# Differential attention two heads at a time: its PE steps put between the halves of a weight chunk, and the vector engine's norm put ahead of two splits

## The chip, the cores and the metric

The kernel runs on one core of a Trainium2 chip. The metric is the device time of one execution in microseconds (us), the median of several runs. Engines are named as the profile names them: PE is the matrix engine and PEld its weight load, DVE the vector engine, ACT the scalar engine, POOL the GpSimd engine, SP the engine that issues most of the weight DMAs.

## What is computed

The reference is a trunk of two layers over 256 tokens of width 2048. Layer 0 mixes tokens by differential attention, layer 1 by dilated sliding-window attention, and each is followed by a gated feed-forward block with a causal convolution. The change touches layer 0's attention and its output projection only:

```python
def diff_attention(h, w_qkv, q_gain, k_gain, lam, subln_g, w_o, rel_bias, layer_idx):
    qkv = h @ w_qkv                                   # 256 x 2048 by 2048 x 6144
    q, k, v = jnp.split(qkv, [nqk, 2 * nqk], axis=-1)
    q = rmsnorm(q.reshape(B, S, N_HEADS, 2, HEAD_DIM), q_gain)
    k = rmsnorm(k.reshape(B, S, N_HEADS, 2, HEAD_DIM), k_gain)
    ...
    logits = q k^T * scale + bias                     # causal, two maps for each head
    p = jax.nn.softmax(logits, axis=-1)
    a = p[:, :, 0] - lam_full * p[:, :, 1]
    o = a @ v
    o = rmsnorm(o, subln_g) * (1.0 - lam_init)
    return o.reshape(B, S, ATTN_WIDTH) @ w_o
```

There are 8 heads with a query and a key of 2 x 128 and a value of 256 columns. Everything is float32, and the products are made to float32 accuracy.

## The kernel before

**How a product is made.** A weight chunk is a slab of 128 partitions x 2048 float32. It lands in one of the four slots of w_raw, ACT rounds it into w_hi (the *high part*, `split_b`, L682, or `split`, L658), and DVE makes the remainder w_lo = w_raw - w_hi (the *low part*, also `split_b`, L1144, or `split`, L1126). The activations xT are kept as a high and a low half in the same way. PE multiplies the high part by both halves of xT (16 matmuls of 512 columns) and then the low part by the high half (8 matmuls). So a plain chunk is 24 matmuls, and it waits twice: for w_hi at its start (`hi_ready`), for w_lo two thirds of the way through (`lo_ready`). A slot of w_raw is loaded again when DVE has made its w_lo; ACT may overwrite w_hi when PE has used the chunk (`used`).

**A pair of heads.** `a_pair` runs over four pairs p = 0 to 3. Each pair has 15 chunks, numbered e = 0 to 14 here as in the code: four "all" chunks for the values (e = 0 to 3, `moving`, matmuls L1902, L1903 and L1909), then eleven for queries and keys (L2053 and L2057). Six of these eleven are mixed as in Strassen's scheme: "one" chunks (9 matmuls) and "sum" chunks (12 matmuls), whose sums of weights DVE makes (`add_weights`, L1162 to L1167). Queries and keys of the two heads come out in four psum banks; after chunk 13 ACT takes one product out (`a_take_p1`, L737), DVE makes four combinations (`a_combine`, L1290 to L1295), and after chunk 14 DVE adds four sums (`a_sum`, L1302). The values come out in two banks after chunk 3 and are scaled into a_v (`a_take_v`: one bank by ACT at L730, the other by DVE at L1281). The lower two banks of chunk 4 can't be written before that (`lower_free` in `upper_first`).

**The attention of pair p - 1 runs beside the chunks of pair p** (`a_attend`, in each engine's program; behind the last pair it runs beside the output projection `a_out_proj`). A_STEPS says after which chunk PE does each of its five steps: transposes of q and k (L1922, waits for `a_qkn`), scores (L1930 and L1933), transposes of the probabilities (L1938), probabilities by values (L1944 to L1946), transposes of the output (L1952). The other engines' parts hang on the same numbers:

```python
A_STEPS = (1, 2, 5, 6, 8)
A_LAST_STEPS = (1, 2, 5, 6, 8)
```

ACT squares the sums at e = 0 (`a_squares`, L744), takes q out at step 0 (L749), does the exponentials at step 1 (`a_exp`, L757) and takes the transposed probabilities at step 2 (L764). DVE normalises q and k at e = 0 (`a_norm`: a reduction at L1307, twelve small instructions, and a product over 128 x 2048 at L1315 that sets `a_qkn`), takes k out at step 0 (L1319), does logits and maxima at step 1 (`a_softmax`, L1331 to L1345), and the weighted difference of the two maps at the entry after it (`a_subtract`).

**Order.** There is no scheduler: each engine's program is written out, and an engine does its instructions in that order. In pair p, ACT and DVE make the parts of chunk e + 3 at entry e (`split_ahead`), before the attention step of that entry. So on DVE the norm (e = 0) stands behind the low part of the pair's chunk 3, and `a_combine` of the pair before stands behind the low part of chunk 1.

**The seam.** `a_out_proj` makes 16 chunks of the output projection: j = 0 to 5 into the left half, 6 to 8 into a third quarter, 9 and 10 left again, 11 third, 12 to 15 the fourth. PE begins it when `a_combined` has come for the last pair. Chunk 9 needs the heads of the last pair, after their transposes (step 4) and `split_o` (L838 on ACT, L1433 on DVE). The third quarter's banks 4 and 5 were also those of the transposed probabilities, so PE waits for `a_aT_ready` ahead of chunk 6.

## Time and profile before

| | us |
|---|---|
| median of 3 runs | 2536.39 (2534.1 to 2538.67) |
| the profiled execution | 2531.31, of which the span is 2529.5 |
| PE busy | 2489.1 (98%) |
| DVE busy | 2165.6 (86%) |
| ACT busy | 1469.0 (58%) |
| DMA | mean 194 GB/s |

The profile is one execution. The span runs from the first to the last instruction; the rest of the execution's time lies around it. Layer 0's attention with its output projection takes the first 440 us of the span; the four pairs' chunks begin at about 24, 77, 161 and 248 us, the output projection at 335 us. PE and PEld overlap. The ends of matmuls are modelled, so a row's idle time can be some tenths of a us short of the distance between two matmuls.

### The profile page before, as it was taken

Reading aid. Unit: us, or ns where it says so; the run is one execution under the profiler, and the core shown is the slowest. Engines: PE = TensorE matmul, PEld = TensorE weight load, DVE = VectorE, ACT = ScalarE, POOL = GpSimd, SP = SyncE. Lnnn points to the kernel's source line nnn. Section 1 sums busy time; section 2 is a strip of 40 time slices with the busy share of each in tenths; the row PEclk is TensorE's granted clock in tenths of the full one; section 3 lists DMA queues with packets and bytes.
Section 4 is the critical chain, followed back from the end, with each engine's and each line's share of the span. In section 5 each row is a group of like instructions: output and inputs, shape, how many; then the busy total and the mean of one; then the engine's idle time right before and its main releaser. Section 6 shows DMA issues by size and latency. Waiting matters only on the chain.

```text
span 2529.5 us, 29120 instructions
## 1 busy us (share of the span) xinstructions
PE 2489.1 (98%) x11403; PEld 2069.2 (82%) x11403; DVE 2165.6 (86%) x2393; ACT 1469.0 (58%) x1432; POOL 44.2 (2%) x54
## 2 busy tenths in 40 slices
PE   9899899999999999999999999999999999999999
PEld 8777777888888888888888888888888888888887
DVE  7777685899999999998787887777599999999998
ACT  6445454767675755565554554544567676665654
POOL 1000000000000000000000000000000000000000
PEclk9999999999999999999999999999999999999999
DMA  8563355567676755665666666555467676755654
GB/s 286 168 195 132 106 183 183 167 221 224 205 231 200 240 177 194 204 224 170 185 185 197 188 185 174 161 162 194 147 213 229 200 239 200 243 189 200 231 172 162
DMA packets 359401, 491.24 MB, mean 194 GB/s; under 512 B 20005, under 2 KB 200437, under 8 KB 356832
## 3 DMA queue, kind: packets, MB, share of 16 engines
q1 hardware_dynamic: 355024, 465.64, 56.1%
q0 software_dynamic: 4000, 23.63, 4.3%
q8 instruction: 90, 1.47, 0.2%
q14 instruction: 47, 0.39, 0.0%
q10 hardware_dynamic: 240, 0.10, 0.0%
HBM read 468.31 MB, written 3.68 MB: 187 GB/s over the span
## 4 chain that ended last, share of the span: by engine, by line
PE 91%; DVE 5%; ACT 2%; issue 1%; DMA 1%; SPq 0%; ACTq 0%; DVEq 0%
PE psum L2053 46%; PE psum L2057 23%; PE psum L1902 5%; PE psum L1903 5%; PE psum L1909 5%; PE psum L2156 2%; DMA w_raw<-in_a_w_qkv 1%; PE psum L2283 1%; DVE w_lo L1144 1%; ACT w_hi L682 1%; PE psum L1922 0%; PE psum L2247 0%; PE psum L2281 0%; PE psum L1860 0%; PE psum L2255 0%
## 5 line engine op out<-in xcount | busy, mean ns | idle before, releaser
L2053 PE MATMUL psum<-w_hi,xT 128*128 128x512 f32 x4456 | 1117.6, 391 | 8.6 <-ACT phase L730 8.6
L2053 PEld LDWEIGHTS psum<-w_hi,xT 128*128 128x128 f32 x4456 | 834.0, 188 | 181.5 <-ACT phase L730 9.8
L669 ACT ACTIVATE w_hi<-w_raw 128x2048 fp32r<-128x2048 f32 (+1 forms) x350 | 631.1, 1810 | 389.6 <-PE psum L2057 257.2
L1136 DVE TENSOR_TENSOR w_lo<-w_raw,w_hi 128x2048 fp32r<-128x2048 f32 (+1 forms) x332 | 705.1, 2145 | 57.4 <-ACT w_hi L669 57.0
L2057 PE MATMUL psum<-w_lo,xT 128*128 128x512 f32 x2228 | 585.1, 390 | 1.0 <-DVE w_lo L1144 0.9
L2057 PEld LDWEIGHTS psum<-w_lo,xT 128*128 128x128 f32 x2228 | 418.8, 188 | 90.1 <-DVE w_lo L1144 2.2
L1144 DVE TENSOR_TENSOR w_lo<-w_raw,w_hi 128x2048 fp32r<-128x2048 f32 (+1 forms) x174 | 376.5, 2178 | 66.8 <-ACT w_hi L682 66.2
L682 ACT ACTIVATE w_hi<-w_raw 128x2048 fp32r<-128x2048 f32 (+1 forms) x174 | 316.0, 1827 | 141.3 <-PE psum L2057 79.5
L2053 PE MATMUL psum<-w_hi,mixT 128*128 128x512 f32 x992 | 265.3, 389 | 0.0
L1902 PE MATMUL psum<-w_hi,xT 128*128 128x512 f32 x624 | 248.9, 399 | 10.2 <-DVE phase L1295 5.0
L1903 PE MATMUL psum<-w_hi,xT 128*128 128x512 f32 x624 | 245.1, 393 | 0.0
L2053 PEld LDWEIGHTS psum<-w_hi,mixT 128*128 128x128 f32 x992 | 186.2, 188 | 38.9
L1909 PE MATMUL psum<-w_lo,xT 128*128 128x512 f32 x624 | 154.2, 389 | 0.0
L1162 DVE TENSOR_TENSOR w_raw<-w_raw 128x1024 f32<-128x1024 f32 x124 | 151.2, 1219 | 2.7 <-DMA w_raw<-in_f_w_down 1.7
L2057 PE MATMUL psum<-w_lo,mixT 128*128 128x512 f32 x496 | 153.1, 390 | 0.0
L1902 PEld LDWEIGHTS psum<-w_hi,xT 128*128 128x128 f32 x624 | 118.6, 190 | 36.9 <-DVE phase L1295 5.4
L1903 PEld LDWEIGHTS psum<-w_hi,xT 128*128 128x128 f32 x624 | 118.7, 190 | 24.0
L1909 PEld LDWEIGHTS psum<-w_lo,xT 128*128 128x128 f32 x624 | 117.1, 188 | 24.3
L1126 DVE TENSOR_TENSOR w_lo<-w_raw,w_hi 128x2048 fp32r<-128x2048 f32 x38 | 86.0, 2288 | 27.9 <-ACT w_hi L658 27.9
L2057 PEld LDWEIGHTS psum<-w_lo,mixT 128*128 128x128 f32 x496 | 92.9, 188 | 20.0 <-DVE w_lo L1144 0.7
L1167 DVE TENSOR_TENSOR w_raw<-w_raw 128x512 f32<-128x512 f32 x124 | 85.8, 692 | 4.2
L1165 DVE TENSOR_TENSOR w_raw<-w_raw 128x512 f32<-128x512 f32 x124 | 85.8, 692 | 4.2
(204 smaller groups left out, 1803.7 us busy)
## 6 DMA issues: line engine op xcount, KB each, us to landing
w_raw<-in_f_w_up SPq DMA_DIRECT2D x352, 512.0 KB, 5.0
w_raw<-in_f_w_down SPq DMA_DIRECT2D x176, 512.0 KB, 5.1
w_raw<-in_b_w_qkv SPq DMA_DIRECT2D x192, 256.0 KB, 3.8
w_raw<-in_a_w_qkv SPq DMA_DIRECT2D x132, 256.0 KB, 4.2
w_raw<-in_b_w_qkv SPq DMA_DIRECT2D x256, 128.0 KB, 2.6
w_lo<-w_raw POOLq DMA_DIRECT2D x18, 1024.0 KB, 7.1
w_raw<-in_a_w_o SPq DMA_DIRECT2D x16, 1024.0 KB, 5.3
w_raw<-in_b_w_qkv SPq DMA_DIRECT2D x32, 512.0 KB, 6.1
```

Of the source, the lines that this page charges most:

```text
L669: nc.scalar.activation(w_hi[:, slot, cols], w_raw[:, slot, cols], ACT.Copy).then_inc(hi_ready, 1)
L682: nc.scalar.activation(w_hi[:, slot, cols], w_raw[:, slot, cols], ACT.Copy).then_inc(hi_ready, 1)
L1126: nc.vector.tensor_tensor(w_lo[:, slot, :], w_raw[:, slot, :], w_hi[:, slot, :], ALU.subtract).then_inc(lo_ready, 1)
L1136: nc.vector.tensor_tensor(w_lo[:, slot, cols], w_raw[:, slot, cols], w_hi[:, slot, cols], ALU.subtract).then_inc(lo_ready, 1)
L1144: nc.vector.tensor_tensor(w_lo[:, slot, cols], w_raw[:, slot, cols], w_hi[:, slot, cols], ALU.subtract).then_inc(lo_ready, 1)
L1162: chain.step(nc.vector.tensor_tensor(t[:, 0:2, :], b[:, 1::2, :], b[:, 0:1, :].to_broadcast([P, 2, 512]), ALU.add))
L1165: chain.step(nc.vector.tensor_tensor(t[:, 2, :], t[:, 0, :], b[:, 3, :], ALU.add))
L1902: pe.matmul(o, xh, hi, start=(first and i == 0), stop=False)
L1903: pe.matmul(o, xl, hi, start=False, stop=False)
L1909: ins = pe.matmul(psum[:, banks[m], 0:n], xT[:, k, 0, P * m:P * (m + 1)], lo, start=False, stop=(last and i == len(blocks) - 1))
L2053: pe.matmul(o, x[:, h, P * m:P * (m + 1)], hi, start=start and h == 0, stop=False)
L2057: return pe.matmul(o, x[:, 0, P * m:P * (m + 1)], part_of(w_lo, c % SLOTS, 512 * tile, 512), start=False, stop=stop)
```

## The change

It has these parts, all in layer 0's attention and output projection:

- **Steps moved.** A_STEPS becomes (2, 3, 5, 6, 8) and A_LAST_STEPS (2, 3, 5, 6, 7): the transposes of q and k and the scores come one chunk later, the last pair's output transposes one chunk earlier. With them go ACT's and DVE's parts.
- **Between the parts of a chunk.** `moving` gets a function `between` that it calls behind the 16 matmuls with the high part and ahead of the wait for the low part. A_BETWEEN and A_LAST_BETWEEN say which steps stand there: the q and k transposes and the scores, and at the seam also probabilities by values.
- **DVE's order at the turn of a pair.** `a_combine` now stands ahead of the low part of chunk 1, that low part stands behind `a_sum`, and the norm stands ahead of the low parts of chunks 2 and 3. For e < 5 the attention step stands ahead of the split, not behind it. At the out projection's j = 0 the norm keeps its place behind the split.
- **a_take_v on ACT alone.** ACT scales both banks, in the place where it scaled one; DVE's instruction is gone.
- **Banks.** The transposed probabilities go to the upper two banks of their four, and PE's wait for `a_aT_ready` ahead of the output projection's chunk 6 is gone.

```diff
-A_STEPS = (1, 2, 5, 6, 8)
-A_LAST_STEPS = (1, 2, 5, 6, 8)
+A_STEPS = (2, 3, 5, 6, 8)
+A_LAST_STEPS = (2, 3, 5, 6, 7)
+A_BETWEEN = (True, True, False, False, False)
+A_LAST_BETWEEN = (True, True, False, True, False)
...
# ACT, a_take_v
-                nc.scalar.activation(a_v[:, p % 2, 0, :], psum[:, a_bank(odd), :], ACT.Copy,
-                                     scale=r_r[:, 0:1]).then_inc(a_v_act, 1)
+                for m in range(M):
+                    ins = nc.scalar.activation(a_v[:, p % 2, m, :], psum[:, a_bank(odd) + m, :], ACT.Copy, scale=r_r[:, m:m + 1])
+                ins.then_inc(a_v_ready, 1)
...
# DVE, a_pair
-                    if e == 3:
-                        a_take_v(c + e, p, odd)
...
-                    if p > 0 or e > 2:
-                        split_ahead(c, e, AO0)
+                    if p > 0 and e < 5:
+                        a_attend(e, p - 1, A_STEPS, 4 - 4 * odd)
+                    if e == A_PAIR - 1:
+                        a_sum(c + e, p, odd)
+                        split_ahead(c, e - 1, AO0)
+                    elif e < A_PAIR - 2:
+                        if p > 0 and e == 0:
+                            split_b(c + LEAD)
+                        if p > 0 or e > 2:
+                            split_ahead(c, e, AO0)
...
-                    else:
+                    elif e >= 5:
                         a_attend(e, p - 1, A_STEPS, 4 - 4 * odd)
...
                     if e == A_PAIR - 2:
                         a_combine(c + A_SUMS[-1], p, odd)
-                    if e == A_PAIR - 1:
-                        a_sum(c + e, p, odd)
...
# DVE, a_out_proj
-                    if j == A_LAST_STEPS[4]:
+                    if j == A_LAST_STEPS[4] + 1:
                         a_take_oT(A_PAIRS - 1, 4)
...
+                    if 0 < j < 5:
+                        a_attend(j, A_PAIRS - 1, A_LAST_STEPS, 4)
                     split(c + j + LEAD)
                     if j < 2:
                         split_o(a_oT, 4 + j)
-                    a_attend(j, A_PAIRS - 1, A_LAST_STEPS, 4)
+                    if j == 0 or j >= 5:
+                        a_attend(j, A_PAIRS - 1, A_LAST_STEPS, 4)
...
# PE, moving
                             pe.matmul(o, xl, hi, start=False, stop=False)
+                if between is not None:
+                    between()
                 pe.wait_ge(lo_ready, lows(c))
...
# PE, a_out_proj
-                    if (what, i) == ("third", 0):
-                        pe.wait_ge(a_aT_ready, A_PAIRS)
```

What this does to the order of instructions is shown at three places. In these rows w_lo<-w_raw,w_hi is the low part of a chunk and w_hi<-w_raw the high part; phase is the memory that holds the attention's tensors. The line numbers differ by a few between the two kernels.

On DVE at the end of a pair, before: the low parts of chunks 13 and 14 and of the next pair's 0 and 1, then `a_combine`, the low part of 2, `a_sum`, the low part of 3, and the norm's reduction.

```order
L1144 TENSOR_TENSOR w_lo<-w_raw,w_hi 128x2048 x4
L1290 TENSOR_TENSOR phase<-psum,phase 128x512
L1292 TENSOR_TENSOR phase<-psum,phase 128x512
L1294 TENSOR_TENSOR phase<-psum,phase 128x512
L1295 TENSOR_TENSOR phase<-phase,psum 128x512
L1144 TENSOR_TENSOR w_lo<-w_raw,w_hi 128x2048
L1302 TENSOR_TENSOR phase<-psum,phase 128x512 x4
L1144 TENSOR_TENSOR w_lo<-w_raw,w_hi 128x2048
L1307 TENSOR_REDUCE small<-phase 128x16
```

The same place in the changed kernel:

```order
L1147 TENSOR_TENSOR w_lo<-w_raw,w_hi 128x2048 x3
L1287 TENSOR_TENSOR phase<-psum,phase 128x512
L1289 TENSOR_TENSOR phase<-psum,phase 128x512
L1291 TENSOR_TENSOR phase<-psum,phase 128x512
L1292 TENSOR_TENSOR phase<-phase,psum 128x512
L1299 TENSOR_TENSOR phase<-psum,phase 128x512 x4
L1147 TENSOR_TENSOR w_lo<-w_raw,w_hi 128x2048
L1304 TENSOR_REDUCE small<-phase 128x16
```

One low part fewer stands ahead of the four combinations, and one stands ahead of the reduction behind them where there were two; the low parts of chunks 2 and 3 have gone behind the norm.

On PE at the transposes of q and k (x16), before: between the low part of chunk 1 (L1909) and the high part of chunk 2.

```order
L1909 MATMUL psum<-w_lo,xT 128x512 x8
L1922 MATMUL psum<-ident,phase 128x128 x16
L1902 MATMUL psum<-w_hi,xT 128x512
L1903 MATMUL psum<-w_hi,xT 128x512
L1902 MATMUL psum<-w_hi,xT 128x512
```

The same place in the changed kernel:

```order
L1906 MATMUL psum<-w_hi,xT 128x512
L1907 MATMUL psum<-w_hi,xT 128x512
L1929 MATMUL psum<-ident,phase 128x128 x16
L1915 MATMUL psum<-w_lo,xT 128x512 x8
L1906 MATMUL psum<-w_hi,xT 128x512
```

The 16 high matmuls of chunk 2 now stand ahead of the transposes, and its low part behind them.

On ACT between taking q out (L749) and the high part of chunk 7, before:

```order
L749 ACTIVATE phase<-psum,gains 128x1024
L682 ACTIVATE w_hi<-w_raw 128x2048
L757 ACTIVATE phase,small<-phase,small 128x256 x4
L757 ACTIVATE phase,small<-phase,small 128x128 x4
L682 ACTIVATE w_hi<-w_raw 128x2048
L730 ACTIVATE phase<-psum,small 128x512
L682 ACTIVATE w_hi<-w_raw 128x1536
```

The same place in the changed kernel:

```order
L752 ACTIVATE phase<-psum,gains 128x1024
L684 ACTIVATE w_hi<-w_raw 128x2048
L733 ACTIVATE phase<-psum,small 128x512 x2
L760 ACTIVATE phase,small<-phase,small 128x256 x4
L760 ACTIVATE phase,small<-phase,small 128x128 x4
L684 ACTIVATE w_hi<-w_raw 128x1536
```

The eight exponentials (L757, now L760) have gone behind the copies of the values (L730, now L733 and two of them), and one high part that stood among them has gone ahead of the copy of q.

## Rows read from the trace of the kernel before

**Rows 1.** The page's part 1: busy time of each engine and its share.

```profile
PE 2489.1 (98%) x11403; PEld 2069.2 (82%) x11403; DVE 2165.6 (86%) x2393; ACT 1469.0 (58%) x1432; POOL 44.2 (2%) x54
```

**Rows 2.** PE's waits: line <- releaser: us in total, times, longest.

```profile
PE psum L1922 <- DVE phase L1315: 14.7, 3, 4.9
PE psum L2053 <- ACT phase L730: 8.6, 3, 2.9
PE psum L1902 <- DVE phase L1295: 5.0, 1, 5.0
PE psum L1902 <- DVE xT L1433: 2.3, 1, 2.3
PE psum L1902 <- DVE phase L1290: 2.0, 3, 0.9
...
PE psum L1902 <- ACT phase L764: 0.9, 1, 0.9
```

**Rows 3.** PE's timeline, last pair: start, us, line, count [idle before <-releaser].

```profile
247.88 0.50 PE L1902 MATMUL psum<-w_hi,xT 128*128 128x512 f32 x1 [0.80 <-DVE phase L1290]
...
257.08 1.98 PE L1909 MATMUL psum<-w_lo,xT 128*128 128x512 f32 x8
263.97 3.39 PE L1922 MATMUL psum<-ident,phase 128*128 128x128 f32 x16 [4.91 <-DVE phase L1315]
```

**Rows 4.** DVE's timeline in the same stretch.

```profile
238.12 9.11 DVE L1144 TENSOR_TENSOR w_lo<-w_raw,w_hi 128x2048 fp32r<-128x2048 f32 x4 [0.31 <-ACT w_hi L682]
247.15 0.68 DVE L1290 TENSOR_TENSOR phase<-psum,phase 128x512 f32<-128x512 f32 x1
...
249.79 2.28 DVE L1144 TENSOR_TENSOR w_lo<-w_raw,w_hi 128x2048 fp32r<-128x2048 f32 x1
252.00 2.48 DVE L1302 TENSOR_TENSOR phase<-psum,phase 128x512 f32<-128x512 f32 x4
...
256.58 2.28 DVE L1307 TENSOR_REDUCE small<-phase 128x16 f32<-128x2048 f32 x1
...
261.62 2.29 DVE L1315 TENSOR_TENSOR phase<-phase,small 128x2048 f32<-128x2048 f32 x1
263.83 2.28 DVE L1144 TENSOR_TENSOR w_lo<-w_raw,w_hi 128x2048 fp32r<-128x2048 f32 x1
```

**Rows 5.** ACT's timeline in the same stretch.

```profile
244.80 0.58 ACT L737 ACTIVATE phase<-psum 128x512 f32<-128x512 f32 x1
...
249.62 1.92 ACT L682 ACTIVATE w_hi<-w_raw 128x2048 fp32r<-128x2048 f32 x1 [1.95 <-DMA w_raw<-in_a_w_qkv]
252.77 2.57 ACT L744 ACTIVATE phase<-phase,small 128x512 f32<-128x512 f32 x4 [1.23 <-DVE phase L1302]
...
284.86 0.67 ACT L730 ACTIVATE phase<-psum,small 128x512 f32<-128x512 f32 x1
```

**Rows 6.** DVE's timeline ahead of the output projection.

```profile
328.30 4.49 DVE L1126 TENSOR_TENSOR w_lo<-w_raw,w_hi 128x2048 fp32r<-128x2048 f32 x2
332.70 0.69 DVE L1290 TENSOR_TENSOR phase<-psum,phase 128x512 f32<-128x512 f32 x1
```

**Rows 7.** Windows: us, busy of PE, PEld, DVE, ACT, POOL (count), granted clock, DMA, GB/s.

```profile
115.00:118.80 3.80, 3.79 (x17) 3.14 (x18) 3.73 (x10) 1.34 (x1) 0.00 (x0) 1.00 0.00 0
...
199.30:203.00 3.70, 3.66 (x9) 2.92 (x10) 3.63 (x9) 1.36 (x1) 0.00 (x0) 0.50 0.02 4
...
264.00:267.10 3.10, 3.10 (x16) 3.10 (x17) 2.12 (x1) 0.00 (x0) 0.00 (x0) 0.53 0.02 5
...
335.50:339.00 3.50, 3.50 (x9) 2.78 (x10) 3.47 (x5) 2.68 (x5) 0.00 (x0) 0.56 0.68 268
348.10:349.90 1.80, 1.78 (x17) 1.78 (x17) 1.80 (x1) 0.00 (x0) 0.00 (x0) 1.00 0.00 0
...
398.50:402.00 3.50, 3.48 (x11) 2.85 (x12) 2.46 (x2) 3.50 (x3) 0.00 (x0) 0.72 0.00 0
```

**Rows 8.** The page's part 6, DMA issues: KB each, median us to landing.

```profile
w_raw<-in_a_w_qkv SPq DMA_DIRECT2D x132, 256.0 KB, 4.2
```

More of the change, by code:

```diff
@@ L763, in a_take_aT @@
                 at_least(act, a_pv, p)
-                nc.scalar.activation(a_aT.rearrange("p (h a) b -> p h (a b)", h=2), psum[:, base:base + 2, 0:3 * P],
+                nc.scalar.activation(a_aT.rearrange("p (h a) b -> p h (a b)", h=2), psum[:, base + 2:base + 4, 0:3 * P],
                                      ACT.Copy).then_inc(a_aT_ready, 1)
@@ L1889, in first_chunk, with moving @@
                 ins.then_inc(used, 1)
-            def moving(c, blocks, n, outs, first, last):
+            def moving(c, blocks, n, outs, first, last, between=None):
                 slot = c % SLOTS
@@ L1911, in moving, with a_attend @@
                 ins.then_inc(used, 1)
-            def a_attend(j, p, steps, base):
-                if j == steps[0]:
+            def a_attend(j, p, steps, base, now):
+                if j == steps[0] and now[0]:
                     pe.wait_ge(a_qkn, p + 1)
@@ L1924, in a_attend @@
                     ins.then_inc(a_tqk, 1)
-                if j == steps[1]:
+                if j == steps[1] and now[1]:
                     pe.wait_ge(a_qT_ready, p + 1)
@@ L1934, in a_attend @@
                     ins.then_inc(a_scores, 1)
-                if j == steps[2]:
+                if j == steps[2] and now[2]:
                     pe.wait_ge(a_diff, p + 1)
                     for i in range(6):
-                        ins = pe.transpose(psum[:, base + i // 3, P * (i % 3):P * (i % 3 + 1)], a_a[:, P * i:P * (i + 1)], ident[:, :])
+                        ins = pe.transpose(psum[:, base + 2 + i // 3, P * (i % 3):P * (i % 3 + 1)], a_a[:, P * i:P * (i + 1)], ident[:, :])
                     ins.then_inc(a_ta, 1)
-                if j == steps[3]:
+                if j == steps[3] and now[3]:
                     pe.wait_ge(a_aT_ready, p + 1)
@@ L1947, in a_attend @@
                     ins.then_inc(a_pv, 1)
-                if j == steps[4]:
+                if j == steps[4] and now[4]:
                     pe.wait_ge(a_on, p + 1)
@@ L1962, in a_entry_of @@
                     else:
-                        moving(c, range(4 * j, 4 * j + 4), 512, [(own, own + 1)], j == 0, j == 3)
+                        moving(c, range(4 * j, 4 * j + 4), 512, [(own, own + 1)], j == 0, j == 3, lambda: a_between(e, p, odd))
                     return
@@ L2008, in a_pair @@
                     else:
-                        a_attend(e, p - 1, A_STEPS, 4 - 4 * odd)
+                        a_attend(e, p - 1, A_STEPS, 4 - 4 * odd, [not now for now in A_BETWEEN])
             splits = [0]
@@ L2023, in a_out_proj, with between @@
                         pe.wait_ge(a_oT_dve, A_PAIRS)
+                    def between():
+                        a_attend(j, A_PAIRS - 1, A_LAST_STEPS, 4, A_LAST_BETWEEN)
                     if what == "left":
                         pe.wait_ge(xs_lo, splits[0] + i + 1)
-                        moving(c + j, (2 * i, 2 * i + 1), 512, [(0, 1), (2, 3)], i == 0, i == 7)
+                        moving(c + j, (2 * i, 2 * i + 1), 512, [(0, 1), (2, 3)], i == 0, i == 7, between)
                     else:
                         pe.wait_ge(xs_lo, splits[0] + 2 * i + 2)
-                        moving(c + j, range(4 * i, 4 * i + 4), 512, [(4, 5) if what == "third" else (6, 7)], i == 0, i == 3)
-                    a_attend(j, A_PAIRS - 1, A_LAST_STEPS, 4)
+                        moving(c + j, range(4 * i, 4 * i + 4), 512, [(4, 5) if what == "third" else (6, 7)], i == 0, i == 3, between)
+                    a_attend(j, A_PAIRS - 1, A_LAST_STEPS, 4, [not now for now in A_LAST_BETWEEN])
                     if j > left and j < left + 3:
```

17 lines of the change are left out of this document (7 added, 10 removed).

## The prediction

> **What bounds the kernel now.** I read the page's part 1 first: PE is busy for 2489.1 of 2529.5 us [rows 1]. No instruction of PE goes away here, so the change can win only what PE doesn't spend at full speed: its 40 us of idle time, and the stretches in which its clock is low. PE's waits say where the idle time lies [rows 2]. Three times 4.9 us ahead of the q and k transposes, which wait for DVE's norm; three times 2.9 us inside chunk 4, which waits for ACT's copy of the values; 5.0 us once where the output projection waits for `a_combine`; 2.3 us once for the last heads' `split_o`; 2.0 us in three at the start of a pair; 0.9 us at the output projection's chunk 6. That is 33.5 us, and the change touches each of these places. The windows add the second part [rows 7]. PE's granted clock is 0.53 in the transposes behind the 4.9 us wait, and 0.56 behind the 5.0 us wait. Behind a 2.9 us wait it was 1.00 one time (115 us) and 0.50 another (199 us).
>
> **The turn of a pair, step by step.** I take the last pair, where PE starts chunk 0 at 247.88 after 0.80 of idle [rows 3]. A plain chunk takes 5.44 us: from 247.88 two of them end at 258.76, about where the L1909 row ends [rows 3]. A high part is two thirds of it, 3.63.
>
> *The combination.* DVE gets to `a_combine` at 247.15, behind four low parts of 9.11 us, and PE's 0.80 wait ends with its first instruction [rows 3, 4]. One low part fewer stands ahead now, which is 9.11 / 4 = 2.28. DVE would be free at 244.87; ACT's copy ends at 244.80 + 0.58 = 245.38 [rows 5]. So it starts at 245.45 and is done 2.64 later (247.15 to 249.79 [rows 4]), at 248.09. Its first instruction ends at 246.13, before PE asks at 247.08. The wait at the start of the pair goes: 2.0 us in three pairs.
>
> *The sums and the norm.* Sums 248.09 to 250.5 (2.4, from 252.00 to the next instruction), low part of chunk 1 to 252.75. PE wants that one only at 247.08 + 5.44 + 3.63 = 256.2. The norm also needs ACT's squares. Here the cover is thin: ACT is on the high part of chunk 3 until 251.5, because its load landed at 249.62, and the four squares take 2.5 more [rows 5]. So they end at 254.0, and the norm starts then and not at 252.75. It takes 263.83 - 256.58 = 7.25 [rows 4]: done at 261.25. PE asks at 247.08 + 10.88 + 3.63 = 261.6. The 4.9 us wait goes, with 0.3 us in hand here and somewhat more in the pairs whose load lands earlier.
>
> *What is late next.* The low parts of chunks 2 and 3 stand behind the norm. The first ends at 261.25 + 2.28 = 263.5; PE needs it after 1.75 us of transposes, at 263.4. The next two low parts and the copy of k (1.28) end at 263.5 + 4.5 + 1.3 = 269.3; PE wants k after 1.81 of low matmuls and 3.63 of high, at 268.9. I book 0.9 us of new waits in this pair and 0.3 in each of the other two: 1.5. Queued behind the waiting transposes is all of PE's work, and DVE's copy of k and ACT's copy of q hang on them.
>
> *Chunk 4.* ACT's copy of the values stood behind eight exponentials; now it stands ahead of them and asks only for chunk 3's end. Two copies take 0.58 + 0.67 = 1.25 us [rows 5], and PE has eight matmuls (1.81) to do before it wants them. The 8.6 us go. The exponentials then start when the maxima are there, as before. In the first pair the two copies end some 0.3 us late, a loss that wasn't there. DVE has four copies less to make, at no gain, since nothing waits for DVE there.
>
> *Loads.* A slot is loaded when its low part is made. Those of chunks 2 and 3 are made later, so chunks 6 and 7 land later. Chunk 6's load is issued at about 263.5, and its high part stands on ACT ahead of the value copies at about 273. A load takes 4.2 us [rows 8]; there are 7 us for it with ACT's 1.9. At nothing, but with this cover.
>
> **The seam.** `a_combine` is at 332.70 behind two low parts of 4.49 [rows 6]. One goes, 2.24: PE starts at 333.3 instead of 335.5. The rest of the 5.0 us stays, some 2.8. The wait for `a_aT_ready` ahead of chunk 6 is gone (0.9). The output transposes come a chunk earlier, 5.44 us, and chunk 9 waited 2.3 for what follows them: gone. The norm's end stays near 347.9 by my sum, and PE, 2.2 us earlier but asking 3.63 later in its own order, waits about 0.3.
>
> **The clock.** Sixteen transposes take 1.78 us at a clock of 1.00 and 3.10 at 0.53 [rows 7]: 1.3 us, three times, is 4.0. At 199.3 us nine matmuls take the 3.7 us in which there are 17 at a clock of 1.00 [rows 7]: (17 - 9) x 0.227 = 1.8, and half as much again until the clock is back, 2.8. In that pair I put 0.6 more for the chunk behind its transposes, which started at a granted clock of a half. Behind the 5.0 us wait 9 matmuls take the time of 15: 1.5. Behind the 2.3 us wait 11 of 15 in the window and as much again after it: 1.7. In all 10.6 at most. Where a wait goes, its low clock goes. The wait of 2.8 us at the seam lies between the rows: I leave its 1.5 in, so 9.1 go.
>
> **The sum.** Gone: 14.7 + 8.6 + 2.0 + 2.2 + 0.9 + 2.3 = 30.7 of idle time and 9.1 of clock. Each wait also costs PE about 0.15 us beyond its idle row, because ends are modelled and the first matmul has to fill: ten waits, 1.5. New: 1.5 in the pairs, 0.3 at the seam, 0.3 in the first pair, 0.3 for eight more changes between kinds of matmul. 30.7 + 9.1 + 1.5 - 2.4 = 38.9; I say **39**. Against the profiled execution that is 2531.3 - 39 = 2492.3. The median of the runs lies 5 us above it, and the runs shown span 4.6; I take the median as the base: 2536.4 - 39 = **2497.4**.
>
> Bounds: if nothing new is waited for and the seam's clock stays up, 2.1 and 1.5 more are won, 43 in all. If the low clock stayed wherever it is now although the waits go (not likely: in 348.10:349.90 sixteen transposes without a wait ran at 1.00), 9.1 less, 30.
>
> **A rule against it.** In 348.10:349.90 the transposes ran at 1.00 between matmuls, and twice as fast as behind a wait [rows 7]. The Trainium skill says otherwise (TensorE: Matmul & The Clock Gate, Part 4: PE-mode transpose): full rate doesn't engage for transposes, since they don't count as work in the same way. By that rule moving them into a chunk would win none of the 4.0 us, and the result would be 35 us. The trace doesn't agree.
>
> **Rivals.**
>
> *The norm is not early enough.* Its start now hangs on ACT's squares, these on the high part of chunk 3, and this on a load with a wait of 1.95 us in front of it [rows 5]. In hand are 0.3 us. Each us by which that load lands later is paid on PE in three pairs, first at the transposes and then at the low part of chunk 2, which stands behind the norm. With 3 us it is 3 x 2.7 = 8 us and perhaps half of the 4.6 us of clock at the transposes: a gain of 29, 2507. For it: the DMA queues are full at this point. Against: that load's slot is freed by chunk 14's low part of the pair before (its wait is where it was), and nothing that is loaded ahead of it moves.
>
> *The clock stays low at more places than I let it*, at the seam and in the pairs, because several short waits stand near each other: 30 to 34 gained, 2502 to 2506.
>
> *Slower than before.* The late loads. If chunk 6's high part isn't there at 273, ACT's value copies stand behind it, PE waits in chunk 4, and behind the copies stand the exponentials, the difference of the maps, and the transposed probabilities. It begins to decide when a load takes over 7 us from issue to ACT's start; every us above is paid three times. To lose more than the 39 us, each load would have to take 7 + 13 = 20 us, and 2 more to be slower by over 0.2%: at 22 us the time is 2542. Against it: 4.2 us in the median [rows 8], and after the turn of a pair the queue has only these loads.
>
> That the change doesn't do what it says is ruled out by the orders shown above: the instructions stand where the sum needs them.
>
> **How the numbers follow.** My sum (gain of 34 to 43): 0.76. The norm late: 0.12. More low clock: 0.08. Slower: 0.02. The remaining 0.02 is a gain near nothing. The likeliest is 2497. The range runs from 43 gained (2493) less 2 for the spread of the runs, 2491, to the rival of the late norm with 2 us beyond it, 2509. A measurement of this kernel can tell about 0.2%, 5 us, from no change. Faster by more than that 0.96, within it 0.02, slower 0.02.
>
> **What would show it.** In PE's waits of the changed kernel the transposes of q and k have under 1 us in any pair, the copy of the values none, and the output projection's start 2.5 to 3 us. The granted clock is 1.00 in the transposes, and each pair takes 73 to 74 us from its first matmul to the next pair's (before, from the starts given with the times: about 84, 87 and 88). In the DVE timeline the norm's reduction starts about 7 us after the pair does, with DVE idle just before it, awaiting the squares. I would be wrong if PE has a new wait of over 1 us for a low part or for k, if ACT waits for the loads of chunks 6 or 7, or if the norm starts over 8 us after the pair.

## The result and the profile after

The changed kernel takes 2490.28 us in the median of four executions (2489.15 to 2490.49), the one before 2536.19 in the executions beside it (2534.1 to 2538.67). The ratio is 0.9818, with a 95% interval of 0.9801 to 0.9835: 45.9 us faster. The prediction said 2497, with a range from 2491. The sign and the places were right, the size was short by 7 us, and the time lies just below the range.

PE's waits of the changed kernel (line <- releaser: us in total, times, longest) answer to [rows 2]:

```profile
PE psum L1906 <- DVE phase L1292: 2.8, 1, 2.8
PE psum L2065 <- ACT phase L733: 1.3, 1, 1.3
PE psum L2389 <- DVE phase L1824: 1.2, 1, 1.2
PE psum L2069 <- DVE w_lo L1147: 1.0, 3, 0.3
```

Of the six waits in [rows 2] one is left, the projection's start with 2.8 us where there were 5.0. The second row is new in its place: it is the copy of the values in the first pair. Of the norm, of k, of a low part behind the norm, PE waits for nothing.

The last pair starts on PE at 224.09 us of the changed kernel. These rows of DVE's timeline from there answer to [rows 4]:

```profile
222.50 0.69 DVE L1287 TENSOR_TENSOR phase<-psum,phase 128x512 f32<-128x512 f32 x1 [0.53 <-issue]
...
225.34 2.48 DVE L1299 TENSOR_TENSOR phase<-psum,phase 128x512 f32<-128x512 f32 x4
227.74 2.28 DVE L1147 TENSOR_TENSOR w_lo<-w_raw,w_hi 128x2048 fp32r<-128x2048 f32 x1
230.57 2.29 DVE L1304 TENSOR_REDUCE small<-phase 128x16 f32<-128x2048 f32 x1 [0.56 <-ACT phase L747]
...
235.62 2.29 DVE L1312 TENSOR_TENSOR phase<-phase,small 128x2048 f32<-128x2048 f32 x1
237.83 6.69 DVE L1147 TENSOR_TENSOR w_lo<-w_raw,w_hi 128x2048 fp32r<-128x2048 f32 x3
244.43 1.28 DVE L1316 TENSOR_SCALAR phase<-psum,gains 128x1024 f32<-128x1024 f32 x1
```

The reduction starts 6.5 us after the pair (predicted: about 7), and DVE idles 0.56 us before it, awaiting ACT's squares (L747), as the chain said. The norm ends at 237.9. On PE:

```profile
238.61 1.91 PE L1929 MATMUL psum<-ident,phase 128*128 128x128 f32 x16
240.27 2.07 PE L1915 MATMUL psum<-w_lo,xT 128*128 128x512 f32 x8
245.86 1.97 PE L1937 MATMUL psum<-phase 128*128 128x256 f32 x8
```

The transposes come without a wait, with 0.7 us in hand (the norm ends at 237.91). The low part of chunk 2 is ready at 240.1 and used at 240.27; k is ready at 245.7 and used at 245.86. So the order fits to some tenths of a us at three places one behind the other.

One of the signs that the prediction had named as being wrong did come, without harm. ACT waits for the load of chunk 6 ahead of its high part:

```profile
246.36 1.91 ACT L684 ACTIVATE w_hi<-w_raw 128x2048 fp32r<-128x2048 f32 x1 [4.69 <-DMA w_raw<-in_a_w_qkv]
250.60 1.27 ACT L733 ACTIVATE phase<-psum,small 128x512 f32<-128x512 f32 x2 [2.32 <-PE psum L1915]
```

The high part is done at 248.3. The copies of the values behind it then wait another 2.3 us for PE's end of chunk 3, so the load cost nothing.

Windows (us, busy of PE, PEld, DVE, ACT, POOL with counts, granted clock, DMA, GB/s) by stage: up to the second pair, the second to the fourth pair (its start wait of the projection included), the projection, the rest. First before:

```profile
0.00:77.45 77.45, 74.90 (x358) 61.97 (x358) 61.31 (x82) 49.42 (x68) 9.28 (x19) 1.00 0.86 289
77.45:160.91 83.46, 74.45 (x337) 61.13 (x338) 62.52 (x80) 40.11 (x53) 0.00 (x0) 0.98 0.47 152
160.91:247.88 86.97, 78.13 (x337) 64.02 (x337) 62.71 (x80) 39.34 (x52) 0.00 (x0) 0.92 0.44 144
247.88:335.48 87.60, 74.53 (x337) 61.23 (x337) 66.82 (x86) 41.82 (x57) 0.00 (x0) 0.98 0.48 158
335.48:440.15 104.67, 101.46 (x458) 83.88 (x459) 65.13 (x84) 48.28 (x70) 0.00 (x0) 0.97 0.48 162
```

and after:

```profile
0.00:78.46 78.46, 75.93 (x358) 63.23 (x359) 60.41 (x82) 50.38 (x69) 9.29 (x19) 1.00 0.87 287
78.46:151.06 72.60, 72.28 (x338) 60.04 (x337) 60.71 (x77) 40.01 (x54) 0.00 (x0) 1.00 0.51 168
151.06:224.09 73.03, 72.71 (x338) 59.99 (x337) 61.66 (x79) 40.04 (x54) 0.00 (x0) 1.00 0.53 174
224.09:299.81 75.72, 72.57 (x338) 59.78 (x336) 65.22 (x84) 43.10 (x59) 0.00 (x0) 1.00 0.53 175
299.81:399.01 99.20, 99.20 (x458) 82.82 (x459) 67.30 (x85) 48.45 (x70) 0.00 (x0) 0.98 0.52 180
399.01:2488.40 2089.39, 2085.59 (x9577) 1736.96 (x9575) 1847.19 (x1984) 1249.53 (x1133) 35.02 (x35) 1.00 0.62 198
```

The differences are -1.0, 10.9, 13.9, 11.9 and 5.5 us: 41.1 in all. The rest of the kernel, 2089.4 us, took 2529.50 - 440.15 = 2089.35 before: nothing was given back there. But 41.1 is the difference of the two profiled executions (2531.3 and 2490.25); the medians differ by 45.9. The 4.8 us between the two is the larger part of what the prediction missed, and the first experiment is on it. By the rows, 30.4 us of the 41.1 are idle time of PE (36.7 us before, 6.3 after) and 10.8 us are busy time (403.5 and 392.7 us for the same work), which is where a low clock shows.

### The profile page after: what moved, and what is told of

It is laid out like the page before. It is cut to its first block, busy times and chain, and to the rows that moved or that the text cites. A ratio compares the mean times of both kernels' runs of the same rounds, so it can differ in the third digit from the quotient of the medians.

```text
span 2488.4 us, 29114 instructions
## 1 busy us (share of the span) xinstructions
PE 2478.3 (100%) x11403; PEld 2062.8 (83%) x11403; DVE 2162.5 (87%) x2389; ACT 1471.5 (59%) x1436; POOL 44.3 (2%) x54
## 3 DMA queue, kind: packets, MB, share of 16 engines
HBM read 468.31 MB, written 3.68 MB: 190 GB/s over the span
## 4 chain that ended last, share of the span: by engine, by line
PE 96%; DVE 2%; ACT 1%; issue 1%; DMA 0%; ACTq 0%
PE psum L2065 48%; PE psum L2069 24%; PE psum L1906 6%; PE psum L1907 6%; PE psum L1915 6%; PE psum L2168 2%; PE psum L2295 1%; PE psum L1864 0%; PE psum L2259 0%; PE psum L2293 0%; PE psum L2267 0%; PE psum L2279 0%; DVE w_lo L1139 0%; ACT w_hi L684 0%; PE psum L2078 0%
## 5 line engine op out<-in xcount | busy, mean ns | idle before, releaser
L2065 PEld LDWEIGHTS psum<-w_hi,mixT 128*128 128x128 f32 x992 | 186.2, 188 | 38.9
L1915 PE MATMUL psum<-w_lo,xT 128*128 128x512 f32 x624 | 155.3, 391 | 0.0
L1915 PEld LDWEIGHTS psum<-w_lo,xT 128*128 128x128 f32 x624 | 116.5, 188 | 24.0 <-DVE w_lo L1147 0.2
```

The lines of the kernel that those rows point to most:

```text
L1915: ins = pe.matmul(psum[:, banks[m], 0:n], xT[:, k, 0, P * m:P * (m + 1)], lo, start=False, stop=(last and i == len(blocks) - 1))
L2065: pe.matmul(o, x[:, h, P * m:P * (m + 1)], hi, start=start and h == 0, stop=False)
```

## Experiments

**Where the median of before gets its 5 us.** The kernel before, unchanged, eleven executions with the mean clock of each, and fifteen more of it beside them.

> The kernel before, unchanged, to see its own executions one by one with their mean clock. The timed runs of before lay at 2534.1 to 2538.7 us and its profiled execution at 2531.3 with a mean clock of 0.995; the changed kernel's executions agree with its profile to 1 us (mean clock 0.999). Theory A, clock luck: executions of before differ by how many of its waits the clock falls behind. Then the longer executions have a lower mean clock: 0.001 of it is 5 us of low clock in 2530, which costs 2.5 us, so 2536 us should show 0.993 and 2538.7 should show 0.992. Theory B, something outside the span or in the DMAs: the mean clock stays at 0.995 in all of them while the times differ by 5 us, or the time lies outside the span (more than the 1.8 us seen).

Measured: 2534.71 us in the median (2533.37 to 2536.11). Mean clocks of 0.992 to 0.993, in none of them the 0.995 of the execution on which the prediction rests. In all the executions of before that ran beside the experiments and in these eleven, 0.995 came twice in 39 (mean 2532.3 us), 0.993 27 times (2534.6), 0.992 nine times (2535.0), 0.991 once (2537.3). The idle rows of this execution are the old ones (14.7, 8.6, 5.0, 2.3 us), but for 2.7 us instead of 2.0 at the starts of the pairs; PE's clock behind them is not the old one. Two of its windows, behind the waits of 2.85 us in chunk 4 of the second and of the third pair:

```profile
117.20:121.00 3.80, 3.75 (x10) 2.98 (x11) 3.73 (x10) 1.37 (x2) 0.00 (x0) 0.56 0.00 0
203.10:207.00 3.90, 3.90 (x9) 3.16 (x10) 3.83 (x10) 1.32 (x1) 0.00 (x0) 0.50 0.01 4
```

In the profile before, the clock was 1.00 at the first of these places and 0.50 at the second [rows 7], and 1.00 behind the third such wait:

```profile
285.50:289.30 3.80, 3.72 (x16) 3.11 (x17) 3.73 (x10) 1.40 (x2) 0.00 (x0) 1.00 0.00 0
```

So the clock fell behind one of the three waits there, and behind two of them here. The pair of the first place took 86.3 us here (78.33 to 164.64) and 83.5 there: 2.85 us more. Another 0.9 us comes from the 78 us ahead of it. These ran at a granted clock of 1.00 both times, so this part isn't clock; 0.5 of it is a longer wait at the start of the second pair (0.82 us against 0.30). With 0.2 us in the third pair that makes the 3.9 us by which the spans differ. So Theory A holds for the larger part: the time outside the span is 1.8 us both times, and most of the difference stands where the clock fell once more. The slope is smaller than I had written (1.2 us for 0.001 and not 2.5); part of the low clock may fall into idle time, which no run shows. Nor does the clock explain all of the spread: the 27 executions with 0.993 lie between 2533.0 and 2536.5 us. The three runs first shown (2534.1 to 2538.7 us) have no clock on record; what of them is clock stays open.

**The value copies alone.** On ACT the exponentials go one entry later, behind the copy of the values; all else as before. A_LAST_STEPS becomes a list of the same numbers, so that the test `steps is A_STEPS` is true in the pairs alone.

```diff
-A_LAST_STEPS = (1, 2, 5, 6, 8)
+A_LAST_STEPS = [1, 2, 5, 6, 8]
...
-                if j == steps[1]:
+                if j == steps[1] + (1 if steps is A_STEPS else 0):
                     a_exp(p)
```

> The kernel before with one edit: on ACT the eight exponentials of a pair stand behind the copy of the values (one entry later), not ahead of it; DVE keeps its bank, all steps of PE stay. My sum prices this part of the change at 8.6 us of idle time and 2.8 us of low clock in the third pair: 11 us faster, 2525, and the waits inside chunk 4 gone. If low clock behind these waits is more common in the timed runs than in the profiled one (three waits, some 2.8 us each where it falls), the gain is 11 to 17. Rival: the exponentials start some 1.5 us later and the difference of the maps with them, so that PE waits for it behind chunk 5 and half the gain goes, 2530.

Measured: 2520.11 us (2519.28 to 2523.36), ratio 0.9945 (0.9932 to 0.9959), 14.6 us faster. The row with 8.6 us is gone from PE's waits and no new one has come. The pairs start at

```profile
78.48 0.50 PE L1902 MATMUL psum<-w_hi,xT 128*128 128x512 f32 x1 [0.66 <-DVE phase L1290]
158.85 0.50 PE L1902 MATMUL psum<-w_hi,xT 128*128 128x512 f32 x1 [0.71 <-DVE phase L1290]
240.16 0.50 PE L1902 MATMUL psum<-w_hi,xT 128*128 128x512 f32 x1 [0.72 <-DVE phase L1290]
```

and in the execution of the first experiment at 78.33, 164.64 and 251.82. So the second and the third pair are 5.9 us shorter each, for 2.85 us of idle time: the two places where that execution had the low clock behind the wait. In all, 8.6 us of idle time took 6 us of clock and refilling with it. That lies in the range of 11 to 17 for more low clock than the one profile showed. The rival, exponentials that come too late, falls.

**DVE's order alone.** The kernel before with DVE's new order at the turn of a pair.

```diff
-                    if p > 0 or e > 2:
-                        split_ahead(c, e, AO0)
+                    if p > 0 and e == 0:
+                        a_attend(e, p - 1, A_STEPS, 4 - 4 * odd)
+                    if e == A_PAIR - 1:
+                        a_sum(c + e, p, odd)
+                        split_ahead(c, e - 1, AO0)
+                    elif e < A_PAIR - 2:
+                        if p > 0 and e == 0:
+                            split_b(c + LEAD)
+                        if p > 0 or e > 2:
+                            split_ahead(c, e, AO0)
...
-                    else:
+                    elif e > 0:
                         a_attend(e, p - 1, A_STEPS, 4 - 4 * odd)
...
-                    if e == A_PAIR - 1:
-                        a_sum(c + e, p, odd)
```

> The kernel before with DVE's new order at the turn of a pair alone: the combinations one low part earlier, the norm ahead of the low parts of chunks 2 and 3; all steps of PE and ACT stay. By my sum the norm ends 14.2 us after the pair's start and PE asks for it at 10.9: the 4.9 us waits shrink to 3.3, the 0.7 us waits at the start of a pair go, the projection's start wait shrinks by 2.2. 3 x 2.3 + 2.2 = 9 us faster, 2527; with less low clock behind the shorter waits up to 13. Rival: the norm can't start earlier since the squares come no earlier, then only 2.2 + 2.0 = 4 us, 2532.

Measured: 2523.62 us (2519.89 to 2525.91), ratio 0.9955 (0.9942 to 0.9969), 11.1 us faster. Its waits for the norm were 3.6, 3.8 and 2.5 us in the pairs (3.3 expected), and there is a new one of 2.1 us at the output projection. The rival, a gain of only 4 us, falls. In the fourth pair, behind 2.5 us, the sixteen transposes took 1.97 us (full clock); behind 3.8 us they took 3.60. The four executions lie at 2520, 2521, 2526 and 2526 with mean clocks of 0.997, 0.997, 0.996 and 0.995: two executions of one program with waits near 3 us differ by 6 us, and the longer ones have the lower clock.

**The steps alone.** The changed kernel with DVE's old order at the turn of a pair.

```diff
-                    if p > 0 and e < 5:
+                    if p > 0 and 0 < e < 5:
                         a_attend(e, p - 1, A_STEPS, 4 - 4 * odd)
-                    if e == A_PAIR - 1:
-                        a_sum(c + e, p, odd)
-                        split_ahead(c, e - 1, AO0)
-                    elif e < A_PAIR - 2:
-                        if p > 0 and e == 0:
-                            split_b(c + LEAD)
-                        if p > 0 or e > 2:
-                            split_ahead(c, e, AO0)
+                    if p > 0 or e > 2:
+                        split_ahead(c, e, AO0)
+                    if p > 0 and e == 0:
+                        a_attend(e, p - 1, A_STEPS, 4 - 4 * odd)
...
+                    if e == A_PAIR - 1:
+                        a_sum(c + e, p, odd)
```

> The changed kernel with DVE's old order at the turn of a pair (norm behind the low part of chunk 3, combinations behind that of chunk 1). PE asks for the norm 14.6 us after the pair's start and it ends at 16.9: waits of 2.3 where the changed kernel has none, 0.7 at the start of each pair, 5.0 at the projection's start. Against before: 8.6 (values) + 3 x 2.6 + 0.9 + 2.3 = 19.6 of idle time, and 6 to 8 of clock: 26 to 28 us faster, 2509, so 19 us slower than the changed kernel. If the clock still falls behind 2.3 us waits: 22 faster, 2514. Together with the DVE order alone (9) that is less than the 46 of the whole: the two work on the same wait, and only the last us of it lets the clock stay up.

Measured: 2498.77 us (2498.55 to 2498.95), ratio 0.9858 (0.9843 to 0.9874), 35.9 us faster. I had expected 26 to 28. PE's waits for the norm (L1927 is the transposes of q and k) and at the start of a pair:

```profile
PE psum L1904 <- DVE phase L1292: 5.0, 1, 5.0
PE psum L1927 <- DVE phase L1312: 3.8, 3, 1.3
PE psum L1904 <- DVE phase L1287: 1.6, 2, 0.9
```

1.3 us each and not 2.3: I had counted PE's start wait of 0.9 us and not taken it off the next one, which it shortens. And the clock stays at 1.00 in the pairs (every window of 40 us from 80 to 280 us) with waits this short. The steps, with the copies of the values that move with them, carry most of the change; with them in place DVE's order brings the last 8 us.

**The two parts of DVE's order, taken back one at a time.** The kernel with the norm taken back, the one with every step behind its chunk and the reordered seam further down ran beside the changed kernel itself; the one with the combinations taken back ran later, beside the kernel before. The changed kernel gave this:

> The changed kernel, unchanged, on the same chip as the three below. Its executions lay at 2489.2 to 2490.5 us. All theories: 2488 to 2491 us with a mean clock of 0.999 to 1.000 in every execution, since one wait of over 2 us is left in it, where the kernel before has nine of 2.3 to 5.0 us and differs by 5 us from one execution to another.

Measured: 2491.03 us (2489.19 to 2494.43), mean clock 0.999 four times, where before lay between 0.991 and 0.995 in the seven executions beside it (2534.43 us). That is a gain of 43.4 us (ratio 0.983, 0.9815 to 0.9844), where the first measurement gave 45.9; the intervals overlap. The two longer ones, 2492.0 and 2494.4, have no lower clock, and I have no profile of them: what makes 5 us between executions at one clock stays open. First the norm, behind the low parts of chunks 2 and 3 again:

```diff
-                    if p > 0 and e < 5:
+                    if p > 0 and 0 < e < 5:
                         a_attend(e, p - 1, A_STEPS, 4 - 4 * odd)
...
                             split_ahead(c, e, AO0)
+                        if p > 0 and e == 0:
+                            a_attend(e, p - 1, A_STEPS, 4 - 4 * odd)
```

> The changed kernel with the norm behind the low parts of chunks 2 and 3 again; the combinations keep their earlier place. By my chain the norm then starts 2.3 to 3.1 us later (two low parts of 2.28 less the 1.5 us for which DVE awaits the squares) and ends 17.4 us after the pair's start, where PE asks at 14.6: three waits of 2.5 to 2.9 us, 8 us slower than the changed kernel, and up to 5 us more where the clock falls behind them: 2498 to 2503. Rival: the low parts themselves, ready earlier, give PE something back; then 6 us slower at most, 2496.

Measured: 2501.77 us (2498.03 to 2507.35), ratio to before 0.9866 (0.9849 to 0.9882): 10.7 us slower than the changed kernel beside it. Its profiled execution:

```profile
PE psum L1931 <- DVE phase L1312: 8.3, 3, 3.2
PE psum L2067 <- ACT phase L733: 4.2, 1, 4.2
```

The norm costs 8.3 us of waits in three pairs (1.9, 3.2 and 3.2), as the chain says. The mean clock is 0.996 to 0.999 in the four executions, and the longer ones have the lower one. The profiled one is the longest, 2507.35 us, and not all of it is the norm: its second pair starts 5.6 us later than in the changed kernel's first profile, behind the 4.2 us wait in the first pair, where this edit changes nothing. The fastest executions differ by 8.8 us, the medians by 10.7, the spans of the profiles without those 5.6 us by 11.6: that part of the change is worth 9 to 12 us. In the median it is slower than the kernel with both parts of DVE's order taken back (2498.77, on another chip). But the two executions with the norm taken back that had a mean clock of 0.999 took 2498.0 and 2500.2 us, about the same: one wait near 3 us in each pair costs PE little more idle time than two of 0.9 and 1.3, and what lengthens the other two executions comes with a lower clock. The second row is the copy of the values in the first pair, which comes back below.

Then the combinations, behind the low part of chunk 1 again, with the norm in its new place:

```diff
                     if e == A_PAIR - 1:
                         a_sum(c + e, p, odd)
-                        split_ahead(c, e - 1, AO0)
-                    elif e < A_PAIR - 2:
+                    elif e < A_PAIR - 1:
```

> The changed kernel with the combinations behind the low part of chunk 1 again; the norm keeps its place ahead of the low parts of chunks 2 and 3. PE waits some 0.8 us at the start of each pair again and 5.0 instead of 2.8 us at the projection's start; the norm's start hangs on ACT's squares, which come as early as now, so no wait is added there: 3 x 0.8 + 2.2 = 4.6 us slower than the changed kernel, and up to 1.6 of clock: 2494 to 2497. Rival: the later combinations push the norm out as well, PE waits another 1 to 2 us in each pair: 2498 to 2501.

Measured: 2494.25 us (2493.17 to 2494.6), ratio 0.9841 (0.9823 to 0.9858). The start wait of the projection is 5.0 us again and there are two waits of 0.8 at pair starts; no wait for the norm. In the second pair DVE idles 2.13 us for ACT's squares ahead of the norm's reduction, which starts 6.7 us after the pair, about as in the changed kernel (6.5 in its last pair). So the norm hangs on the squares and not on the combinations, and this part is worth 3 to 4 us, by executions that did not run beside each other. The rival falls.

**Between the parts, or behind the chunk.** All of A_BETWEEN and A_LAST_BETWEEN False: each step behind its chunk.

> The changed kernel with no step between the parts of a chunk: the same steps (2, 3, 5, 6, 8 and 2, 3, 5, 6, 7), each behind its chunk. PE asks for the norm, for k and for q 1.8 us later, so nothing new is waited for there. The scores come 1 us later, and with them the exponentials and the difference of the maps, which then ends at the very time at which PE asks for it. My theory, that the chunk of distance does the work and the place within the chunk is worth little: 0 to 1.5 us slower, 2490 to 2492. Rival, that the place between the parts is needed: the difference comes 1 to 2 us late in each pair and the seam, 4 to 8 us slower, 2494 to 2498.

Measured: 2498.41 us (2496.56 to 2506.87), ratio 0.9864 (0.9844 to 0.9884): 7.4 us slower than the changed kernel in the median (two executions at 2496.6, one at 2500.2, one at 2506.9 with a mean clock of 0.997). My theory fell, and the profile says by what:

```profile
PE psum L1915 <- DVE w_lo L1147: 5.6, 3, 2.3
...
PE psum L1945 <- DVE phase L1356: 2.7, 3, 0.9
```

PE waits for the low part of chunk 2 (L1915), 1.6 to 2.3 us in each pair. That low part stands behind the norm on DVE. The transposes between the parts are 1.75 us of other work for PE in just the time in which DVE makes it. I had used this cover in my own prediction (263.4 against 263.5) and forgotten it in this expectation. The second row is the difference of the maps, 0.9 us late in each pair: the rival's mechanism, but with 2.7 us of waits for the 4 to 8 that it said. The larger wait stood in neither theory.

**A better seam.** The remaining 2.8 us. For the last pair ACT takes its product out ahead of one high part, DVE makes the combinations ahead of the low part of the projection's chunk 0, and the norm stands ahead of the low part of chunk 2.

```diff
# ACT, a_pair
+                    if p == A_PAIRS - 1 and e == A_PAIR - 2:
+                        a_take_p1(c + A_ONES[-1], p, odd)
                     if p > 0 or e > 0:
                         split_ahead(c, e, AO0)
...
# DVE, a_pair
-                        if p > 0 or e > 2:
+                        if (p > 0 or e > 2) and not (p == A_PAIRS - 1 and e == A_PAIR - 3):
                             split_ahead(c, e, AO0)
...
                         a_combine(c + A_SUMS[-1], p, odd)
+                        if p == A_PAIRS - 1:
+                            split_ahead(c, e - 1, AO0)
...
# DVE, a_out_proj
-                    if 0 < j < 5:
+                    if j < 5:
                         a_attend(j, A_PAIRS - 1, A_LAST_STEPS, 4)
...
-                    if j == 0 or j >= 5:
+                    if j >= 5:
                         a_attend(j, A_PAIRS - 1, A_LAST_STEPS, 4)
```

> The changed kernel with the seam ordered as the turns of the pairs: for the last pair ACT takes its product out ahead of the high part of the projection's chunk 1, DVE makes the combinations ahead of the low part of its chunk 0 too, and the norm stands ahead of the low part of chunk 2. The last wait of 2.8 us shrinks by one low part to 0.6, and the low clock behind it (0.83 between 300 and 310 us) goes: 2.2 + 1.6 = 3.8 us faster than the changed kernel, 2486. Rival: the norm then comes late by what was gained, since PE asks 2.2 us earlier; with the norm ahead of one low part it has 2.3 us in hand, so at most 1 us of that. If the chain is held by ACT's copy, nothing is won, 2490.

Measured: 2487.29 us (2486.01 to 2489.52), ratio to before 0.9814 (0.98 to 0.9829), 3.7 us faster than the changed kernel beside it (3.2 between the fastest executions). The wait is 0.6 us (L1910), nothing of size has taken its place, and the mean clock is 1.000 in three of four executions:

```profile
PE psum L2393 <- DVE phase L1828: 1.2, 1, 1.2
PE psum L2073 <- DVE w_lo L1149: 0.9, 3, 0.3
PE psum L1910 <- DVE phase L1294: 0.6, 1, 0.6
```

Run again, beside the next kernel:

> The kernel with the reordered seam, unchanged, beside the two above on one chip: 2485 to 2488 us as before, with a wait for the values in the first pair of 0 to 4 us that differs from one execution to the next. All theories say the same.

Measured: 2486.6 us (2485.76 to 2487.01), ratio 0.981 (0.9792 to 0.9827). It beats the kernel before and the changed one. Its profile has no wait for the values in the first pair, but one of 0.9 us for the norm in the last pair, where the seam's order changes nothing: the close call at that place does not always go well.

**The first pair.** The changed kernel's profile has a wait of 1.3 us for the value copies in the first pair, its second profile (h0_changed) 0.2, the kernel with the norm taken back 4.2. The copies stand on ACT behind the high part of chunk 6, and that hangs on a load. In the last of these it landed late (ACT's timeline of the kernel with the norm taken back):

```profile
38.37 1.91 ACT L684 ACTIVATE w_hi<-w_raw 128x2048 fp32r<-128x2048 f32 x1 [4.92 <-DMA w_raw<-in_a_w_qkv]
40.18 1.25 ACT L733 ACTIVATE phase<-psum,small 128x512 f32<-128x512 f32 x2
```

In the changed kernel's first profile the row reads

```profile
35.54 1.92 ACT L684 ACTIVATE w_hi<-w_raw 128x2048 fp32r<-128x2048 f32 x1 [2.10 <-PE psum L1915]
```

It names PE, which ended chunk 3 just then. But in the second profile of the same program this high part began at 34.29 us, before chunk 3 ended (35.4), so it doesn't wait for that. In the code it waits for its load and for the end of chunk 2. That the load was late here too is inferred from this and not read from a row.

The kernel with the better seam, and the copies ahead of that high part:

```diff
+                    if e == 3:
+                        a_take_v(c + e, p, odd)
                     if p > 0 or e > 0:
                         split_ahead(c, e, AO0)
-                    if e == 3:
-                        a_take_v(c + e, p, odd)
```

> The kernel with the reordered seam, and on ACT the copy of the values also ahead of the high part of chunk 6, not behind it. In the first pair that high part hangs on a load that landed at 33.6 to 38.4 us in the runs so far, and PE's wait for the values there was 0.0 to 4.2 us; now the copy hangs on no load. The wait of the first pair is gone in all executions: 0 to 1 us faster than the seam alone in the median and closer together, 2484 to 2487. Rival: the load itself holds PE one or two chunks later (the high part of chunk 6), then no gain.

Measured: 2487.26 us (2486.83 to 2489.87), ratio 0.9815 (0.9799 to 0.983). The wait is gone from the profile, but the time is 0.7 us longer than that of the seam alone beside it, and not closer together. In the profile of the seam alone beside it the load was early (34.1 us) and PE had no wait for the values, so there the edit had nothing to win; whether it would have helped in an execution with a late load is not shown.

## Why the prediction fell short

*Right, by its own steps.* PE's waits and the low clock behind them as the whole of the gain; the combinations one low part earlier; the norm's start held by the squares, with DVE idle before it; the copies of the values in time in the later pairs; the loads covered, though ACT did wait for that of chunk 6; the projection's start at 2.8 us; the pairs at 72.6 and 73.0 us, where 73 to 74 was forecast; the transposes at full clock. In window 92.90 to 94.70 of the changed kernel sixteen of them ran at a granted clock of 1.00, so the rule of the Trainium skill that was weighed (TensorE: Matmul & The Clock Gate, Part 4: PE-mode transpose) doesn't hold here, as the earlier row had said. All three rivals fell. One sign was missed: the copies of the values should have cost PE no wait, and cost 1.3 us in the first pair.

*The step that failed: the base, and in the sum the clock behind the copies of the values.* I took 39 us off the median although the 39 were worked out on one execution, and wrote the 5 us between the two off as spread. But the sum used that execution's clock. It had the clock low behind one of the three 2.85 us waits, and the sum books 2.8 us for it. The execution of the first experiment had it low behind two of them and took 2.85 us more in that pair, and the edit that takes these three waits away and nothing else won 14.6 us in the median where the sum has 8.6 + 2.8 = 11.4. In all but two of 39 executions of before the mean clock was under the 0.995 of the profiled one. The changed kernel has none of these waits, and its mean clock is 0.999 to 1.000 in eight of eight executions. So taking waits away takes away the loss of an average execution, and that was some 3 us more than the one I costed.

The rest of the 4.8 us between the two differences is not shown to be clock. The execution of the first experiment also lost 0.9 us in the first 78 us, at a clock of 1.00. And the median of before was 2536.2 us beside the result and 2534.4 to 2534.7 in the three sets beside the experiments, for a reason that no run shows. In the second measurement of the changed kernel the gain is 43.4 us and not 45.9: up to 2.5 us of the miss can be the luck of one set of executions. The signs were in sight: the three runs shown all lay above the profiled execution, and [rows 7] had one wait of one length with both clocks behind it. The Trainium skill says of the start of a kernel (TensorE: Matmul & The Clock Gate, Part 1, What's actually happening) that the same kernel shows different numbers of slow matmuls from one run to the next. Here the same was seen behind a wait in mid-kernel: a clock of 1.00 in one execution and 0.56 in another.

*Terms that were mis-sized.* In the profiled executions the sum said 38.9 and 41.1 was measured. New waits: 2.1 booked (1.5 in the pairs, 0.3 at the seam, 0.3 in the first pair), 1.3 came, all of it in the first pair, where the load was probably late; in the pairs every one of the close calls went well in this execution. Clock and refilling: 9.1 + 1.5 booked less 0.3 for changes between kinds of matmul; what is left of 41.1 after 30.7 of idle time and 1.3 of new wait is 11.7. That number is a remainder; the stage windows show 10.8 us less busy time and 30.4 us less idle time. The part that can be read from rows fits: the transposes of the three pairs took 3.3, 3.7 and 3.4 us before and 1.9 each after, 4.6 us less, as booked (4.0 and 0.6). The 0.15 us for each wait's refilling is isolated by no run. The low end of the range, 43 gained on the median, would have had to be 43 on the profiled execution plus those 5 us: 2488.

## What to carry to other kernels

Where PE stands several times for 2.5 to 5 us, count each wait at its length plus the slow stretch behind it, and take the slow stretch from several executions and not from one: the value copies alone were 8.6 us of idle time and 14.6 us of time. If the median lies above the profiled execution and the change removes waits, suspect that part of the gap goes too. Work that waits for another engine belongs between two parts of a product that don't need it, and what stands behind it on the other engine (here the low part of the same chunk) may be what that place really covers. Taken back alone, the place between the parts gave back 7 us of the 43 here, and the norm's place on DVE 9 to 12.

## What the runs showed of the hardware

Behind waits of 2.85 us PE's granted clock was 1.00 in some cases and 0.50 to 0.56 in others, at the same place of the same program. At the q and k transposes it was 0.50 behind a wait of 3.20 us and 1.00 behind one of 3.17 us in one execution (178 and 257 us of the kernel with the norm taken back), and behind 2.54 us they ran at full speed. Shorter waits were not free of it: 0.79 in the 2.5 us behind a wait of 1.93 us in the same execution, and 0.72 in the 3.5 us behind the 2.3 us wait of the projection [rows 7]. Sixteen transposes took 1.91 to 1.97 us at the full clock (2.4 GHz), and 3.27 to 3.68 us behind waits of 4.9 us at a granted clock of 0.50 to 0.56, near the half one (1.2 GHz). And the high part of one chunk in the crowded first 40 us began on ACT at 33.6 to 38.4 us in programs that issue its load alike, mostly behind a wait for that load, and PE's wait on what stands behind it went from 0 to 4.2 us.
